# A decoder step on Trainium2: sample attention with keys turned by the vector engine and scores in quarters of the array

## What is computed

```python
z = jnp.einsum('bqhd,bkhd->bhqk', qb, kb) * scale + bias
log_beta = jax.nn.log_sigmoid(z)
log_keep = jnp.where(mask, log_beta - z, 0.0)
rest = lax.cumsum(log_keep, axis=3, reverse=True) - log_keep
a = jnp.where(mask, jnp.exp(log_beta + rest), 0.0)
outs.append(jnp.einsum('bhqk,bkhd->bqhd', a, vb))
```

## Time and profile before

| what | value |
|---|---|
| median of 3 runs | 3729.41 us (3727.08 to 3733.83) |
| the profiled execution, its own time | 3737.79 us |
| its span (first to last instruction) | 3736.1 us |
| PE, DVE, ACT, POOL busy | 3210.8, 1885.8, 937.8, 610.8 us |
| mean granted PE clock | 0.946 of full speed |

### The profile page before, as it was taken

One profiled execution on the slowest core, in us unless ns is written; L12 is line 12 of the kernel. 1 busy time (PEld: TensorE's weight loads), 2 busy tenths in 40 slices (PEclk: granted clock), 3 DMA queues, 4 the chain that ended last, 5 costly groups with the idle time before them and its releaser, 6 DMA issues. The chain is left out here.

```text
span 3736.1 us, 57991 instructions
## 1 busy us (share of the span) xinstructions
PE 3210.8 (86%) x20912; PEld 2718.3 (73%) x20912; DVE 1885.8 (50%) x3138; ACT 937.8 (25%) x1598; POOL 610.8 (16%) x528
## 2 busy tenths in 40 slices
PE   5655999999995979788888887888885999999997
PEld 1235999999985979555555555444484999999996
DVE  2566555555543121344444444888815555555554
ACT  0113000000012010333333333777714100000003
POOL 0002222212101111122222221000010222222210
PEclk7887999999997989899999998999997999999998
DMA  8702111111101220798888886000010211111101
GB/s 323 261 29 62 46 45 45 40 43 42 39 0 58 88 63 26 284 351 341 337 350 334 340 339 225 22 19 23 6 45 0 68 45 45 45 45 45 45 22 48
DMA packets 215604, 432.70 MB, mean 116 GB/s; under 512 B 13664, under 2 KB 130057, under 8 KB 212441
## 3 DMA queue, kind: packets, MB, share of 16 engines
q1 hardware_dynamic: 215521, 431.67, 31.7%
HBM read 417.92 MB, written 13.92 MB: 116 GB/s over the span
## 5 line engine op out<-in xcount | busy, mean ns | idle before, releaser
L84 PE MATMUL bank<-hi,mlp_uphi 128*128 128x364 f32 (+1 forms) x1536 | 506.9, 330 | 92.2 <-POOL mlp_uplo L697 92.2
L85 PE MATMUL bank<-lo,mlp_uphi 128*128 128x364 f32 (+1 forms) x1536 | 506.7, 330 | 0.0
L86 PE MATMUL bank<-hi,mlp_uplo 128*128 128x364 f32 (+1 forms) x1536 | 506.6, 330 | 0.0
L85 PE MATMUL bank<-mlp_flo,mlp_dnhi 128*128 128x364 f32 (+1 forms) x1536 | 504.7, 329 | 0.0
L86 PE MATMUL bank<-mlp_fhi,mlp_dnlo 128*128 128x364 f32 (+1 forms) x1536 | 504.7, 329 | 0.0
L84 PE MATMUL bank<-mlp_fhi,mlp_dnhi 128*128 128x364 f32 (+1 forms) x1536 | 504.6, 329 | 0.0
L307 DVE SCALAR_TENSOR_TENSOR x_t<-bank,mod,x_t 128x364 f32<-128x364 f32 (+1 forms) x432 | 245.5, 571 | 379.7 <-PE bank L86 377.4
L84 PEld LDWEIGHTS bank<-hi,mlp_uphi 128*128 128x128 f32 x1536 | 290.5, 189 | 93.4 <-POOL mlp_uplo L697 93.4
L697 POOL TENSOR_TENSOR mlp_uplo<-mlp_raw,mlp_uphi 128x1024 fp32r<-128x1024 f32 x64 | 162.5, 2540 | 827.3 <-ACT mlp_uphi L682 423.3
L85 PEld LDWEIGHTS bank<-lo,mlp_uphi 128*128 128x128 f32 x1536 | 290.5, 189 | 0.0
L86 PEld LDWEIGHTS bank<-hi,mlp_uplo 128*128 128x128 f32 x1536 | 290.3, 189 | 0.0
(11 more groups left out here) (255 smaller groups left out, 5652.7 us busy)
## 6 DMA issues: line engine op xcount, KB each, us to landing
sa_kpage<-in_cache_k SPq DMA_DIRECT2D x256, 512.0 KB, 6.4
sa_vpage<-in_cache_v SPq DMA_DIRECT2D x256, 512.0 KB, 6.1
mlp_raw<-in_w_up SPq DMA_DIRECT2D x64, 512.0 KB, 4.0
mlp_raw<-in_w_down SPq DMA_DIRECT2D x64, 512.0 KB, 3.5
w_raw<-in_w_ada SPq DMA_DIRECT2D x24, 1024.0 KB, 8.6
pm_wada<-in_w_ada SPq DMA_DIRECT2D x48, 512.0 KB, 5.2
kv_raw<-in_w_kv SPq DMA_DIRECT2D x8, 1024.0 KB, 5.5
x_rows<-in_x_prompt SPq DMA_DIRECT2D x1, 4096.0 KB, 13.4
```

Source lines behind the costliest of these rows:

```text
L84: pe.matmul(out, w_hi, x_hi, start=start, stop=False, skip_group_check=True)
L85: pe.matmul(out, w_hi, x_lo, start=False, stop=False, skip_group_check=True)
L86: return pe.matmul(out, w_lo, x_hi, start=False, stop=stop, skip_group_check=True)
```

## The change

- K pages are turned by DVE and no longer by PE: one `dve.transpose` of 128 by 1,024 for each page, which transposes each block of 32 by 32 by itself. Key groups of 32 so stay on their quarter of the partitions, and each 64-wide head is split into two halves of 32.
- `scores(n)` is 128 matmuls in place of 8. Each has a weight of 32 rows by 32 columns and 128 moving columns, and sits at one of 16 positions of the array (row quarter `r`, column quarter `g`). Each row quarter writes its own PSUM bank `Z[r]`.
- ACT adds the bias in four copies of 128 columns (before: one DVE instruction of 512).
- The softplus sums run on: DVE makes `c_run` by four dependent additions of 128 columns for a unit, and `subtract_sums` needs 6 matmuls in place of 10. POOL's sums in each unit are gone. It now makes four small tiles once in a sequence.
- All loops but SP's are unrolled over the 64 units `n`, and units overlap across sequences: two output banks `OA`, two query tiles `q_w`, which DVE fills during the sequence before in 16 copies. The weights `att` have one buffer in place of two.
- The first K pages are issued at the start of the stage (DVE raises `turned` by `EARLY_K` at once), while the new keys are still worked on. Two reductions of 128 by 1,024 and the 16 query copies of the first sequence are added to DVE's part there.

The diff, cut to the loops (tiles, semaphores, POOL's four tiles and the setup are left out):

```diff
+        Z, ZT, OA = k.ps[0:4], [k.ps[4], k.ps[5]], [k.ps[6], k.ps[7]]
         npages = a["cache_k"].shape[0]
+        EARLY_K, EARLY_V = 8, 2
...
-                        sp.wait_ge(k_turned, b * TURNS + (2 * (n + 25) if n < 8 else 2 * (n - 7) + TURNS))
-                        sp.dma_start(k_pages[u % 2][:, g, :], kc[bass.ds(page[n], 1), :, :].rearrange("n p d -> (n p) d")
+                        sp.wait_ge(turned, b * (4 * UNITS) + (4 * u - 4 + EARLY_K))
+                        sp.dma_start(k_raw[u % 2][:, g, :], kc[bass.ds(page[n], 1), :, :].rearrange("n p d -> (n p) d")
                                      ).then_inc(k_in[n % 8], 16)
...
-                        sp.wait_ge(v_used, b * UNITS + (u + 6))
+                        sp.wait_ge(v_used, b * UNITS + (u - 2 + EARLY_V))
                         sp.dma_start(v_page[:, n % 8, :], vc[bass.ds(page[n], 1), :, :].rearrange("n p d -> (n p) d")
                                      ).then_inc(v_in[n % 8], 16)
...
+            flat = t[:, :, :].rearrange("p g n -> p (g n)")
+
+            def softplus_of_negative(n):
+                act.wait_ge(z_done, n + 1)
+                act.wait_ge(zt_done, n)
+                for r in range(4):
+                    act.activation(z_rows[:, :, r, :],
+                                   Z[r][:, P * (n % 2):P * (n % 2) + P].rearrange("p (x j) -> p x j", j=32),
+                                   ACT.Identity, bias=k.bias_row[:, 0:1]).then_inc(z_kept, 1)
+                act.wait_ge(zt_done, n + 1)
+                act.wait_ge(c_done, 4 * n)
+                act.activation(flat, ZT[n % 2][:, :], ACT.Abs).then_inc(abs_done, 1)
+                act.wait_ge(abs_done, n + 1)
+                act.activation(flat, flat, ACT.Exp, scale=-1.0).then_inc(e_done, 1)
+                act.wait_ge(e_done, n + 1)
+                act.activation(flat, flat, ACT.Ln, bias=1.0).then_inc(l_done, 1)
+
+            softplus_of_negative(0)
+            for n in range(W):
+                if n + 1 < W:
+                    softplus_of_negative(n + 1)
+                act.wait_ge(tri_done, n + 1)
+                if n:
+                    act.wait_ge(v_used, EARLY_V + n)
+                act.activation(att[:, :, :].rearrange("p g n -> p (g n)"), ZT[n % 2][:, :], ACT.Exp).then_inc(a_done, 1)
 
         @block.vector
         def _(dve):
             new = Tally(dve, dve_new)
+            dve.sem_inc(turned, EARLY_K)
...
+            def ready_queries(b, g):
+                if b == 0 and g == 0:
+                    dve.wait_ge(q_zeroed, 2)
+                if b >= 2:
+                    dve.wait_ge(z_done, UNITS * (b - 1))
+                rows = slice(32 * g, 32 * g + 32)
+                for par in range(2):
+                    for half in range(2):
+                        src = 64 * par + 32 * half
+                        dve.tensor_copy(
+                            q_w[b % 2][rows, :, half, :].rearrange("p g (h s) -> p g h s", h=4)[:, :, par::2, 0:DS],
+                            k.q_t[src:src + 32, :, TP + b * DS:TP + b * DS + DS].rearrange("p (g r) q -> p g r q", r=2)
+                            ).then_inc(q_ready, 1)
+            for g in range(4):
+                ready_queries(0, g)
             dve.wait_ge(trin_done, 1)
             for j in range(2):
...
+            def turn_keys(n, x):
+                if n >= W:
+                    return
+                if x == 0:
+                    if n >= 2:
+                        dve.wait_ge(z_done, n - 1)
+                dve.wait_ge(k_in[4 * (n % 2) + x], 16 * (n // 2 + 1))
+                dve.transpose(k_t[n % 2][:, x, :], k_raw[n % 2][:, x, :]).then_inc(turned, 1)
+
+            def finish(b):
+                dve.wait_ge(v_used, EARLY_V + UNITS * (b + 1))
+                own = OA[b % 2][:, 4 * HD:8 * HD]
+                dve.tensor_tensor(own.rearrange("p (h d) -> p h d", h=4),
+                                  OA[b % 2][:, 0:4 * HD].rearrange("p (h d) -> p h d", h=4),
+                                  over(k.block_of[:, :], HD), ALU.mult).then_inc(o_part_done, 1)
+                dve.wait_ge(o_part_done, b + 1)
+                dve.tensor_reduce(o_rows[:, b, :], own.rearrange("p (h d) -> p d h", h=4), AX.X, ALU.add
+                                  ).then_inc(o_row, 1)
+
+            for n in range(2):
+                for x in range(4):
+                    turn_keys(n, x)
+            for n in range(W):
+                b, u = divmod(n, UNITS)
+                flat = t[:, :, :].rearrange("p g n -> p (g n)")
+                dve.wait_ge(l_done, n + 1)
+                dve.scalar_tensor_tensor(flat, ZT[n % 2][:, :], 0.0, flat, ALU.max, ALU.add).then_inc(sp_done, 1)
+                dve.wait_ge(sp_done, n + 1)
+                if n:
+                    dve.wait_ge(lo_done, n)
+                for g in range(4):
+                    if g:
+                        dve.wait_ge(c_done, 4 * n + g)
+                        before = c_run[:, g - 1, :]
+                    elif u:
+                        before = c_run[:, 3, :]
+                    else:
+                        dve.wait_ge(new_ready, 2 * b + 1)
+                        before = sp_b[:, :]
+                    dve.tensor_tensor(c_run[:, g, :], before, t[:, g, :], ALU.add).then_inc(c_done, 1)
+                c_all = c_run[:, :, :]
+                dve.wait_ge(c_done, 4 * n + 4)
+                if n:
+                    dve.wait_ge(tri_done, n)
+                dve.tensor_copy(c_hi[:, n % 2, :, :], c_all).then_inc(hi_done, 1)
+                dve.wait_ge(hi_done, n + 1)
+                dve.tensor_tensor(c_lo[:, n % 2, :, :], c_all, c_hi[:, n % 2, :, :].bitcast(F32), ALU.subtract
+                                  ).then_inc(lo_done, 1)
+                for x in range(4):
+                    turn_keys(n + 2, x)
+                if u == 1 and b:
+                    finish(b - 1)
+                if 2 <= u < 6 and b + 1 < DB:
+                    ready_queries(b + 1, u - 2)
+            finish(DB - 1)
+            dve.wait_ge(o_turned, 2)
             for j in range(2):
...
+            def scores(n):
+                b = n // UNITS
+                pe.wait_ge(turned, EARLY_K + 4 * n + 4)
+                if n >= 2:
+                    pe.wait_ge(z_kept, 4 * (n - 1))
+                if n % UNITS == 0:
+                    pe.wait_ge(q_ready, 16 * (b + 1))
+                for hh in range(4):
+                    for half in range(2):
+                        for r in range(4):
+                            for g in range(4):
+                                d0 = HD * (4 * g + hh) + 32 * half
+                                last = pe.matmul(
+                                    Z[r][32 * g:32 * g + 32, P * (n % 2):P * (n % 2) + P].rearrange("p (x j) -> p x j", j=32),
+                                    q_w[b % 2][32 * r:32 * r + 32, g, half, 32 * hh:32 * hh + 32],
+                                    k_t[n % 2][32 * r:32 * r + 32, :, d0:d0 + 32],
+                                    start=(hh == 0 and half == 0), stop=(hh == 3 and half == 1),
+                                    tile_position=(32 * r, 32 * g), skip_group_check=True)
+                last.then_inc(z_done, 1)
+
+            def turn_scores(n):
+                pe.wait_ge(z_kept, 4 * n + 4)
+                if n >= 2:
+                    pe.wait_ge(a_done, n - 1)
+                for x in range(4):
+                    last = pe.matmul(ZT[n % 2][:, P * x:P * x + P], z_rows[:, x, :, :].rearrange("p r j -> p (r j)"),
+                                     k.ident[:, :], start=(x == 0), stop=False, is_transpose=True, skip_group_check=True)
+                last.then_inc(zt_done, 1)
+
+            def subtract_sums(n):
+                b, u = divmod(n, UNITS)
+                zt = ZT[n % 2][:, :].rearrange("p (g n) -> p g n", g=4)
+                pe.wait_ge(lo_done, n + 1)
+                if u == 0:
+                    pe.wait_ge(new_ready, 2 * b + 1)
+                for half, new in ((c_hi, pn_hi), (c_lo, pn_lo)):
+                    pe.matmul(zt, k.neg_tri[:, :], half[:, n % 2, :, :], start=False, stop=False, skip_group_check=True)
+                    pe.matmul(zt[:, 1:4, :], k.neg_above[:, :], half[:, n % 2, 0:3, :], start=False, stop=False,
+                              skip_group_check=True)
+                    last = pe.matmul(zt[:, 0, :], k.neg_above[:, :], half[:, 1 - n % 2, 3, :] if u else new[:, :],
+                                     start=False, stop=(half is c_lo), skip_group_check=True)
+                last.then_inc(tri_done, 1)
+
+            def add_values(b, weight, v, start, stop):
+                for q in range(4):
+                    last = pe.matmul(OA[b % 2][32 * q:32 * q + 32, 0:4 * HD], weight[:, 32 * q:32 * q + 32],
+                                     v[:, 256 * q:256 * q + 256], start=start, stop=stop,
+                                     tile_position=(0, 32 * q), skip_group_check=True)
+                return last
+
```

(90 more changed lines are left out.)

250 lines of the change are left out of this document (43 added, 207 removed).

## The result

The changed kernel takes 3942.4 us (median of 4 runs, 3926.6 to 3945.5) against 3728.3 (4 runs, 3727.1 to 3733.8): ratio 1.0563, 95% interval 1.0532 to 1.0593. The forecast of 3617 was wrong in sign.

A forecast was written before the change was run, and what follows sets the result against it. Page transfers were to bound at 10.2 us a unit, ending the stage at 2186 instead of 2310.9: 125 us saved, less 12 for transfer gaps, gives 113 and a median of 3617; range 3602 to 3830.

The forecast's parts named there:

- the last sentence on queued work: Sample attention, PE's code: about 600 unrolled instructions a unit, 2.5 MB in all, priced at 6 us of transfers.
- Scores, 2.3 us: PE's scores in each unit: 256 pairs of load and matmul take 2.3 us, with ends of 2.0 and 12.5.
- the 5.6 that the forecast named as a sign of being wrong: Scores of a unit taking over 5.6 us would mean PE is the bound and DMA falls under 340 GB/s.
- PE issues too slowly: Rival for the scores: 29 ns a pair, 7.4 us, unit 13.9 us, total 3841; chance 0.16.
- 1.2 us a page: DVE's transpose of one K page: 1.2 us, so 4.8 us of DVE's 8.6 us a unit.
- The chain, 6.5 us plus scores: Dependent steps from one unit's logarithm on DVE to the next: 6.5 us plus scores, 8.8 us in all.
- Transfers at 10.2 us as the bound: Page loads of 4.19 MB a unit at about 412 GB/s take 10.2 us and become the stage's bound.
- K(n+2) behind it for a buffer that is long free: SP's issue order V(n), K(n+2): K's buffer is free early, up to eight pages outstanding, engines don't run dry.
- No gap at a sequence's end: Sign of being right in the profile after: transfers show no gap where one sequence ends and the next starts.
- T(0), 1539: Start of the stage: DVE has unit 0's logarithm at 1539, from first turning near 1528, plus 4.8, 2.3 and 3.9.
- Clock and a longer chain: Rival, small gain: clock 0.73 makes the unit 10.6 us, 3640; with slower scores 3660 to 3720; chance 0.18.
- DVE at half pace: Rival for DVE's page transposes: 2.45 us a page, 13.6 us a unit, total 3822; chance 0.06.

The follow-up runs named there:

- the plain forms: Changed kernel with all units on sequence 0's queries and one output bank, new key in unit 0 only: PE written out 3956.2 us, PE from a loop 3677.9 us.
- looped: Changed kernel with sequence 0's queries and one output bank for all units, and PE's units 2 to 61 from a loop over two units: 3677.9 us.
- experiment 5: Changed kernel with PE in a two-unit loop, sequence 0's queries for all units, and each page transposed twice by DVE: 3833.1 us.
- the best form: Changed kernel, all work done, PE in a two-unit loop, K(8b) issued ahead of V(8b-1), SP's loop written out: 3663.3 us, ratio to before 0.9817.
- the new order: Changed kernel, all work done, PE in a two-unit loop, SP issuing K(8b) ahead of V(8b-1): 3686.4 us with SP looped, 3663.3 with SP written out.

## Why the prediction was wrong, step by step

**The step that failed** is the last sentence on queued work: "Unrolled PE code is about 600 instructions of 64 bytes a unit, 2.5 MB in all, 6 us of transfers". The bytes were right (144 more packets of 16 KB, 2.4 MB). The price was that of their share of the bandwidth. What counts is the time to the next block: PE uses up 128 pairs in 1.8 us at full pace (128 times 13.7 ns), and a block came only every 6.2 us with full loads beside it. That was no rival, and so the sum, all rivals and the range were built on a PE that always has its code. The stops and the low clock that went with them cost 278 us between the plain forms.

**Where the 15 us of a unit come from.** From 2000.07 to 2015.19 it is 15.1 us: 2.6 of stop, 1.7 more for `values` (3.64 against 1.93), 0.4 for the turning (1.11 against 0.66 looped) and 0.5 for scores at a slower pace (2.68 and 1.37 against 3.58); without these 9.9, the looped unit. The next, of 16.2 us, has 0.82 and 2.59 of stops. Over the window of 960 us the waits for issue add up to 187 us, 2.9 a unit. So somewhat over half is stops; the rest goes with the low clock (`values` at 3.64 us is nearly twice 1.93).

**Scores, 2.3 us.** Mis-sized: 3.5 with the code at hand, 13.7 ns a pair. The burst of 10 ns didn't last. In the changed kernel one unit's scores last 6.7 us from start to end (2000.07 to 2006.76), over the 5.6 that the forecast named as a sign of being wrong, but 2.6 of them are a stop. Without stops they stay under 5.6, so the rival "PE issues too slowly" was wrong in its mechanism, although its 13.9 us a unit and 3841 us came nearest. The Trainium skill's 25 ns floor ("TensorE: Matmul & The Clock Gate") isn't seen in the loop.

**DVE** 1.2 us a page: right (1.215). DVE waited for the keys only 78 us in the whole stage.

**The chain, 6.5 us plus scores:** right; 9.91 looped with scores of 3.58, where the sum gives 10.1.

**Transfers at 10.2 us as the bound:** right once PE has its code, 10.4 at 398 to 402 GB/s for the forecast's 412.

**SP, "K(n+2) behind it for a buffer that is long free":** right inside a sequence, wrong at its boundary, where V(8b-1) stands ahead of K(8b). "No gap at a sequence's end" was therefore wrong: 15.5 - 9.9 = 5.6 us in the looped form shown; in the changed kernel, slow as it was, hidden (PE waited for turned keys 4.5 us in its whole window).

**T(0), 1539.** DVE's first use of the logarithm came at 1543.33; the first scores had a stop of 2.09 us for code in them.

**Rivals.** Clock and a longer chain: the clock did fall, to 0.72 where 0.73 was assumed, but with the stops, which the rival didn't have, and without them the chain was 9.9. That the number met is luck. DVE at half pace: experiment 5 makes it true and gives 13.5 us a unit and 3833, for the 13.6 and 3822 worked out. That sum's arithmetic holds; what it lacked was a term.

Of the 46 us between 3617 and the best form, the 0.2 us a unit explain 13; the code written out ahead of and behind the loop still has stops (one of 2.60 us in the last scores at 2214), and the tail with the new keys ends at 2240.7 where 2186 stood. The rest was not divided up.

## What to carry to other kernels

Count an engine's instructions per microsecond before writing its code out. Where an engine uses up 256 instructions faster than a block arrives (here 1.8 us against 3.5 to 4.0 alone and 6.2 beside full page loads, start to start), put the work in a loop whose body stays resident, and move what differs between the turns to engines with little code. For SP the opposite helped once: in the new order each jump back left 10 us without an issue, and straight code took them away; in the kernel before and in the changed one, where q14 had 40 and 50 packets, it changed nothing. Many small instructions have a price that no busy time shows: the rows to look for are "issue" waits at places without a semaphore, and the packets of the instruction queues. The word "issue" alone proves nothing: the kernel before has 60.9 us of it at its scores, behind semaphores, and just as much (60.3) with its loop written out.

## What was not expected of the hardware

- PE stops for code in pieces of exactly 128 pairs, 0.66 to 1.20 us with quiet DMA engines and 3.40 us beside loads at 407 GB/s.
- A loop of about 2,400 PE instructions (4033 us) is slower than the same code written out (3956); one of about 1,200 takes 3678.
- 256 pairs on 16 positions run at 13.7 to 13.8 ns a pair at full clock and go on so for 30 sets (7,670 recorded pairs in 106 us).
- With a stop at each block the clock stood at 0.50 over 100 us in which PE did nothing but these matmuls.
